# Hybrid two-layer trunk, one core: the odd layer's triangular inverse in 32x32 blocks, both output gates whole on ScalarE, and one output factor in the weight rows

## The reference

```python
m = jnp.where(strict, betac[..., :, None] * kk * gam, 0.0)          # 64x64, strictly lower, per head and chunk
rhs = jnp.concatenate([vc * betac[..., None], kc * (betac * jnp.exp(bc))[..., None]], axis=-1)
sol = lax.linalg.triangular_solve(m + jnp.eye(CHUNK), rhs, left_side=True, lower=True, unit_diagonal=True)
...
o = rms_norm(o, out_gain) * jax.nn.silu(z)                          # mixer C, gate z
o = head_group_norm(o, d_gain, d_bias) * jax.nn.silu(g)             # mixer D (retention), gate g
return jnp.concatenate([o_c, o_d], axis=-1) @ w_out
```

## Time and profile before

| | |
|---|---|
| median of 3 runs | 586.52 us (586.25 to 588.19) |
| profiled execution | 586.91 us, of which its span (first to last instruction) 584.7 us |
| granted TensorE clock, mean | 0.975 |
| PE busy over the span | 541.3 us (93%) |
| DVE, ACT, POOL busy | 328.9, 254.0, 81.4 us |
| DMA | 144.16 MB, mean 247 GB/s |
| inverse, levels 1 to 6 (first line 2467 to last 2490) | about 363.8 to 405.4 us |
| first output projection unit | 420.31 us |

### The profile page before, as it was taken

The page is one execution under the profiler, slowest core; times in us unless marked ns, Lnnn a source line. Parts: engine busy times, 40 slices in busy tenths (PEclk is TensorE's granted clock), DMA queues, the critical chain, the costliest instruction groups (busy, mean ns, idle before and its releaser), DMA issues.

```text
span 584.7 us, 12159 instructions
## 1 busy us (share of the span) xinstructions
PE 541.3 (93%) x5162; PEld 445.5 (76%) x5162; DVE 328.9 (56%) x595; ACT 254.0 (43%) x501; POOL 81.4 (14%) x98
## 2 busy tenths in 40 slices
PE   6999799999899999789999999999999889999975
PEld 6999799996565645359989998999889656664632
DVE  3579876657334333377996555467445633334335
ACT  5576467664233323155546434433226323331311
POOL 5716621100000000021003900011110000000000
PEclk9999999998999999999999799999789989999999
DMA  9991333787899999997463430000315979989992
GB/s 319 272 371 58 108 109 110 228 305 295 312 408 409 375 411 409 390 376 243 160 215 80 176 109 2 4 4 2 145 34 225 411 282 411 408 347 412 407 409 109
DMA packets 55671, 144.16 MB, mean 247 GB/s; under 512 B 4292, under 2 KB 29088, under 8 KB 55488
## 3 DMA queue, kind: packets, MB, share of 16 engines
q1 hardware_dynamic: 54496, 141.88, 64.6%
q0 software_dynamic: 944, 1.41, 1.2%
q10 hardware_dynamic: 176, 0.07, 0.1%
HBM read 142.30 MB, written 1.05 MB: 245 GB/s over the span
## 4 chain that ended last, share of the span: by engine, by line
PE 75%; DVE 14%; ACT 5%; issue 3%; POOL 1%; DMA 1%; ACTq 0%; DVEq 0%
PE PS L2097 11%; PE PS L2058 7%; PE PS L2119 6%; PE PS L610 6%; PE PS L611 5%; PE PS L612 5%; PE PS L2133 4%; PE PS L646 3%; DVE WL L606 3%; PE PS L648 2%; PE PS L647 2%; PE PS L2134 2%; PE PS L2467 2%; PE PS L2488 2%; DVE SL L1303 2%
## 5 line engine op out<-in xcount | busy, mean ns | idle before, releaser
L606 DVE TENSOR_TENSOR WL<-RAW,WH 128x768 fp32r<-128x768 f32 (+2 forms) x90 | 82.0, 947 | 30.2 <-ACT WH L592 29.8
L610 PE MATMUL PS<-WH,HTH 128*128 128x384 f32 (+2 forms) x272 | 93.2, 343 | 3.0 <-DVE HTL L1295 1.4
L611 PE MATMUL PS<-WL,HTH 128*128 128x384 f32 (+2 forms) x272 | 90.1, 331 | 0.0
L612 PE MATMUL PS<-WH,HTL 128*128 128x384 f32 (+2 forms) x272 | 90.0, 331 | 0.0
L1295 DVE TENSOR_TENSOR X<-PS,X 128x512 f32<-128x512 f32 (+2 forms) x84 | 53.9, 663 | 48.0 <-PE PS L2134 36.1
L592 ACT ACTIVATE WH<-RAW 128x768 fp32r<-128x768 f32 (+2 forms) x90 | 67.2, 793 | 4.8 <-PE PS L612 3.1
L610 PEld LDWEIGHTS PS<-WH,HTH 128*128 128x128 f32 x272 | 53.5, 197 | 4.4 <-DVE HTL L1295 1.7
L611 PEld LDWEIGHTS PS<-WL,HTH 128*128 128x128 f32 x272 | 53.7, 197 | 0.0
L992 ACT ACTIVATE SIL<-PS,MW 128x128 f32<-128x128 f32 x18 | 6.6, 367 | 107.6 <-PE PS L2097 98.0
L612 PEld LDWEIGHTS PS<-WH,HTL 128*128 128x128 f32 x272 | 53.3, 196 | 0.0
L646 PE MATMUL PS<-HTH,WH 128*128 128x256 f32 x160 | 46.0, 287 | 0.4 <-DVE HTL L1303 0.4
(11 more groups left out here) (362 smaller groups left out, 1060.8 us busy)
## 6 DMA issues: line engine op xcount, KB each, us to landing
RAW<-moe_w_down SPq DMA_DIRECT2D x32, 512.0 KB, 13.1
RAW<-moe_w_gate SPq DMA_DIRECT2D x32, 512.0 KB, 7.8
RAW<-moe_w_up SPq DMA_DIRECT2D x32, 512.0 KB, 8.6
XD<-moe_w_down SPq DMA_DIRECT2D x32, 512.0 KB, 13.4
XG<-moe_w_gate SPq DMA_DIRECT2D x32, 512.0 KB, 9.2
XG<-moe_w_up SPq DMA_DIRECT2D x32, 512.0 KB, 10.3
RAW<-od_w_in SPq DMA_DIRECT2D x9, 1536.0 KB, 7.8
RAW<-ev_w_in SPq DMA_DIRECT2D x5, 1536.0 KB, 15.4
```

The source lines that it names most:

```text
L606: done(nc.vector.tensor_tensor(out=lo, in0=raw, in1=hi.bitcast(F32), op=ALU.subtract), "unit_lo")
L610: nc.tensor.matmul(ps, ah, bh, start=start, stop=False)
L611: nc.tensor.matmul(ps, ah, bl, start=False, stop=False)
L612: return nc.tensor.matmul(ps, al, bh, start=False, stop=stop)
```

## The change

Three edits.

**The inverse.** Levels 1 to 4 work on 32x32 blocks, four to a column of 128 partitions (`quarters`), so that a call loads 32 columns of weights. Only half of a block's columns is needed as the right factor (`first_half`), 16 columns. The products of a level no longer depend on each other in a row: the transposes and the products of `NTD` with `YC` are issued together (`inverse_TQ`), one ACT copy of 128x384 takes both (`inverse_X`), and one product follows (`inverse_Z`). Two small masked copies (`placed`) bring it into `YC`. Level 0 now has a product of its own (`inverse_N`). Level 5 puts 64x64 blocks together with calls of 32 or 64 columns; level 6 (`inverse_last`, `inverse_last_Z`) keeps 64x64 calls and additionally transposes all of `YC` into `UT`, which ACT copies in quarters (`inverse_upper`). `solved` is then one 128x64 call per head instead of two. The two groups are staggered by one level.

**The gates.** ACT takes Silu of the whole gates; DVE no longer forms them.

**The factor.** Mixer C's gain is loaded as a column (`CCOLG`) and multiplied into the rows of the output weights when they are split; `CGAIN` and its DVE multiplication go. The table of masks grows from 7 to 10 slices.

```diff
@@ masks, split of the weights
+    lower = np.stack([upper[0:CH, n, 0:CH].T for n in range(6)], 1)
+    lower = np.concatenate([lower, lower], 0).reshape(P, 3, P)
+    return np.concatenate([upper, lower], 1).astype(np.float32)
...
+            if plan[i][:2] == (1, "out") and j < 2:
+                return CCOLG
...
@@ GpSimd
+            for i in range(NT):
+                link(nc.gpsimd.memset(UT[CH:P, 2 * i, :, 0:CH], 0.0), also="c_uz")
...
-                link(nc.gpsimd.tensor_copy(YS[CH:P, :, hs, :], YC[CH:P, :, hs, :]), also="c_ys")
@@ ScalarE
             def inverse_X(g, L):
-                rows = slice(0, P if L < 6 else CH)
                 act.wait_ge(sem(f"c_T{g}"), L)
-                done(nc.scalar.activation(heads(XC, g)[rows], level_ps(0, g)[rows], ACT.Copy), f"c_X{g}")
-
-            def inverse_Q(g, L):
-                rows = slice(0 if L < 6 else CH, P)
-                act.wait_ge(sem(f"c_Q{g}"), L)
-                done(nc.scalar.activation(heads(QC, g)[rows], level_ps(2, g)[rows], ACT.Copy), f"c_Qs{g}")
+                done(nc.scalar.activation(XC[:, g, :], PS[:, g, 0:384], ACT.Copy), f"c_X{g}")
...
+            def inverse_upper(g, c):
+                act.wait_ge(sem(f"c_T{g}"), 6)
+                rows = slice(CH * c, CH * c + CH)
+                done(nc.scalar.activation(UT[rows, 0::2, 4 * g:4 * g + 4, rows],
+                                          PS[rows, g, :].rearrange("p (h i t) -> p i h t", h=4, i=2), ACT.Copy), f"c_Qs{g}")
...
-            done(nc.scalar.activation(SG[:, :, :], TM[:, :, 0:512], ACT.Tanh, scale=0.5), "gate_t")
+            done(nc.scalar.activation(SG[:, :, :], TM[:, :, 0:512], ACT.Silu), "gate_t")
@@ VectorE
+            def placed(g, L, b):
+
+                c = 2 ** (L + 1)
+                for half in range(2):
+                    cols = slice(32 * half, 32 * half + 32)
+                    to = YC[:, 4 * g:4 * g + 4, :, cols].rearrange("p h i (m c) -> p (h i) m c", c=c)[:, :, :, 0:c // 2]
+                    m1 = MKC[:, L, cols].rearrange("p (m c) -> p m c", c=c)[:, :, 0:c // 2]
+                    z = PS[:, b, 0:128].rearrange("p (n m c) -> p n m c", n=8, c=c // 2)
+                    done(nc.vector.copy_predicated(to, m1.unsqueeze(1).to_broadcast([P, 8, 32 // c, c // 2]), z), f"c_Y{g}")
...
-            link(stt(tg, tg, 1.0, TM[:, :, 1552:2064], ADD, MUL))
-            link(stt(SG[:, :, :], SG[:, :, :], 1.0, TM[:, :, 0:512], ADD, MUL))
-            link(stt(g16, g16, 0.5, bc(CGAIN, 1, [P, 16, 64]), MUL, MUL))
@@ TensorE
+            def inverse_TQ(g, L):
+                pe.wait_ge(sem(f"c_Y{g}"), 2 * L)
+                if L < 5:
+                    for n, (i, h) in enumerate(group(g)):
+                        for q, rows in enumerate(quarters):
+                            mm(PS[rows, g, 32 * n:32 * n + 32], inverse_block(q, i, h), ident[rows, rows], start=True, stop=True)
+                    for n, (i, h) in enumerate(group(g)):
+                        o = 256 + 16 * n
+                        for q, rows in enumerate(quarters):
+                            last = mm(PS[rows, g, o:o + 16], key_block(q, i, h), first_half(inverse_block(q, i, h), L),
+                                      start=True, stop=True)
...
+            def inverse_Z(g, L):
+                pe.wait_ge(sem(f"c_X{g}"), L)
...
+                        for q, rows in enumerate(quarters):
+                            last = mm(PS[rows, 2 + 2 * g, 16 * n:16 * n + 16], XC[rows, g, 32 * n:32 * n + 32],
+                                      XC[rows, g, 256 + 16 * n:256 + 16 * n + 16], start=True, stop=True)
...
-                    mm(PS[low, 2 * i + g, hs], YC[low, i, h, :], rhs[low, h, :], start=True, stop=True)
-                    last = mm(PS[high, 2 * i + g, hs], YS[:, i, h, :], rhs[:, h, :], start=True, stop=True)
+                    last = mm(PS[:, 2 * i + g, hs], UT[:, 2 * i, h, :], rhs[:, h, :], start=True, stop=True)
```

More of the change, by code:

```diff
@@ L591, in split_hi, with row_gain @@
             raw, hi, _ = unit_views(i, j)
-            done(nc.scalar.activation(hi, raw, ACT.Copy, scale=BCOLG if scaled(i, j) else 1.0), "unit_hi")
-        def scaled(i, j):
-            return plan[i][:2] == (0, "out") and j >= 2
+            gain = row_gain(i, j)
+            done(nc.scalar.activation(hi, raw, ACT.Copy, scale=1.0 if gain is None else gain), "unit_hi")
+        def row_gain(i, j):
+            if plan[i][:2] == (0, "out") and j >= 2:
+                return BCOLG
+            if plan[i][:2] == (1, "out") and j < 2:
+                return CCOLG
+            return None
         def split_lo(dve, i, j):
@@ L1870, in _ @@
             inverse_level(0, 1)
+            first_level(1)
+            inverse_level(0, 2)
             inverse_level(1, 1)
@@ new lines, in _, with first_half, key_block, inverse_block @@
+            quarters = [slice(32 * q, 32 * q + 32) for q in range(4)]
+            def first_half(a, L):
+                return a.rearrange("p (m c) -> p m c", c=2 ** (L + 1))[:, :, 0:2 ** L]
+            def key_block(q, i, h):
+                return NTD[quarters[q], h, 256 * i + 32 * q:256 * i + 32 * q + 32]
+            def inverse_block(q, i, h):
+                return YC[quarters[q], h, i, 32 * (q % 2):32 * (q % 2) + 32]
+            def inverse_N(g):
+                pe.wait_ge(sem("c_nt"), 2 * g + 1)
+                for n, (i, h) in enumerate(group(g)):
+                    for q, rows in enumerate(quarters):
+                        last = mm(PS[rows, g, 16 * n:16 * n + 16], key_block(q, i, h), first_half(ident[rows, rows], 0),
+                                  start=True, stop=True)
+                done(last, f"c_N{g}")
@@ new lines, in inverse_Z, with inverse_last @@
+                done(last, f"c_Z{g}")
+            def inverse_last(g):
+                pe.wait_ge(sem(f"c_Y{g}"), 12)
+                for n, (i, h) in enumerate(group(g)):
+                    last = mm(PS[high, 2 + 2 * g, CH * n:CH * n + CH], NTD[low, h, 256 * i + CH:256 * i + P], YC[low, h, i, :],
+                              start=True, stop=True)
+                done(last, f"c_Q{g}")
+                for n, (i, h) in enumerate(group(g)):
+                    for rows in halves:
+                        last = mm(PS[rows, g, CH * n:CH * n + CH], YC[rows, h, i, :], ident[rows, rows], start=True, stop=True)
+                done(last, f"c_T{g}")
@@ L2491, in inverse_Z, with inverse_last_Z @@
+            def inverse_last_Z(g):
+                pe.wait_ge(sem(f"c_Qs{g}"), 2)
+                for n, (i, h) in enumerate(group(g)):
+                    last = mm(PS[low, 3 + 2 * g, CH * n:CH * n + CH], QC[high, g, n, :], UT[high, 2 * i, h, CH:P], start=True, stop=True)
                 done(last, f"c_Z{g}")
@@ L2531, in _ @@
             pe.wait_ge(sem("proj_ev"), proj_total[1])
+            inverse_N(0)
             key_scores(1)
+            inverse_TQ(0, 1)
             retention_scores(1)
[L2534 to L2547 removed]
+            pe.wait_ge(sem("c_nt"), 2)
+            inverse_Z(0, 1)
+            inverse_N(1)
+            inverse_TQ(0, 2)
+            inverse_TQ(1, 1)
+            retention_out()
+            inverse_Z(0, 2)
+            inverse_Z(1, 1)
+            inverse_TQ(0, 3)
+            inverse_TQ(1, 2)
+            inverse_Z(0, 3)
+            inverse_Z(1, 2)
+            values_T()
+            inverse_TQ(0, 4)
+            inverse_TQ(1, 3)
+            inverse_Z(0, 4)
+            inverse_Z(1, 3)
+            query_scores(0)
+            inverse_TQ(0, 5)
+            inverse_TQ(1, 4)
+            inverse_Z(0, 5)
+            inverse_Z(1, 4)
+            query_scores(1)
+            inverse_last(0)
+            inverse_TQ(1, 5)
+            inverse_last_Z(0)
+            inverse_Z(1, 5)
+            query_scores(2)
+            inverse_last(1)
             first_rows(0)
+            query_scores(3)
+            inverse_last_Z(1)
+            residue(0, 1)
             first_rows(1)
             pe.wait_ge(sem("c_at"), 4)
+            outputs(0, 0, 1)
+            second_rows(0)
+            residue(1, 2)
             lhs(mixed, lambda i: pe.wait_ge(sem("d_mix"), 1), D_PIECES)
[L2552 to L2555 removed]
             outputs(1, 0, 3)
```

216 lines of the change are left out of this document (97 added, 119 removed).

## The result

The changed kernel is slower: 605.9 us median of 6 runs (596.2 to 615.7) against 586.4 for the kernel before, ratio 1.0218 with a 95% interval of 1.017 to 1.0266. Forecast were 574 us and a range of 568 to 593. A second comparison on another chip gave 1.0186 (1.0108 to 1.0265).

A forecast was written before the change was run, and what follows sets the result against it. PE, issuing the inverse's products without a gap, was taken as the bound. Savings 16.3 - 1.7 - 2.0 + 2.2, plus 1.1 for the last solve, less 3.0 and 0.3, left 12.6 off 586.9: 574 us, range 568 to 593.

The forecast's parts named there:

- what a 32x32 call costs: Inverse on PE: a 32x32 call (two records) takes 15.5 ns with four corners, against 58.5 ns a call before.
- how fast PE takes records in: PE's intake, read from 48 layer 0 records on four corners: 24 ns a record or less.
- the 10.6 us to be saved: Levels 1 to 4 of the inverse: 5.62 us a level becomes 2.98, saving 4 x 2.64 us.
- Rival 2: Inverse: PE takes narrow records no faster than today; 58.5 ns a call, 608 us, or 50 ns, 601; chance 0.10.
- Corners: Inverse: the four diagonal 32x32 blocks run beside each other in the array, as four 64x64 corners do in layer 0.
- Rival 3: Inverse: only two corners run side by side, 29.3 ns a call, 582 us; chance 0.11.
- The clock: Before the first output unit: 3.0 us allowed for a clock fall; fails if at 0.50 for over 7 us.
- Rival 1: Small products leave PE so empty that its clock stays at 1.2 GHz through the inverse; 592 us, chance 0.12.
- Levels 0 and 5, the solve: PE: level 0 adds 1.0 us; level 5 falls from 5.62 to 2.4; each solve from 2.05 to 0.84 to 0.9.
- Copies: Inverse: ACT's 384-column copy takes 0.47 us, DVE's small masked copy of 128 elements 0.30.
- Rival 4: Inverse waits for DVE: a small masked copy takes 0.73 us, giving 581 us; chance 0.05.
- The rest: Outside the inverse: gates' table load hidden, gain folding 0 to 0.1 us, larger masks at the start cost 0.3 us.

The follow-up runs named there:

- the kernel in 64x64 calls: Changed kernel's order, transposed inverse, one-call solve and gates, but 64x64 calls at all levels; 1.0002 of the kernel before.
- 160 further calls: Kernel before plus 160 64x64 calls into idle array corners in the T (transpose) steps of levels 1 to 5, results unread; 1.0097 of the kernel before.
- 464 further calls: Kernel with 64x64 calls at all levels plus 464 calls into idle corners in T, Q and Z steps, results unread; 603.6 us, 1.0286 of the kernel before.
- half of the blocks: Changed kernel without the odd 32-row corners in levels 0 to 4, so half the blocks are not inverted; 577.7 us, 0.9925 of the kernel before.
- the values' transposes later: 64x64-call kernel with VectorE transposes, its TensorE transposes of the values moved behind the Q steps of levels 4 and 3; 0.9983 of the kernel before.

## Why the prediction was wrong, by its steps

- **The step that failed** is the cost of a call, 15.5 ns, under "what a 32x32 call costs", at "how fast PE takes records in: 24 ns or less, no more". The nearest row was 48 records long, 96 instructions: less than one packet. It could show the pace of a burst and nothing on the pace over 4000 instructions. In a burst at a clock of 1.00 the 15.5 was nearly right: at 380.35 us, 62 records of L2503 take 0.72 us and one alone 0.19, 8.7 ns apart, 17.4 a call. Sustained, a call is four instructions of 13.6 to 14.0 ns: 54.5 to 56 ns. At that price the 768 calls of levels 1 to 4 are 42 to 43 us (an estimate), where the 384 before were 22.5 and 11.9 were forecast: the 10.6 us to be saved became a loss.
- **The count** of instructions was never made. Between the last input product and the first output product TensorE has 2509 instructions before and 4317 after. At 14.0 ns the latter are 60 us by themselves, as long as the whole stretch was (61.1), so nothing was left to save. The trace of before does not show the limit, though: in it TensorE never stands still for want of a packet, and its packets start 3.7 us apart at the closest from 363 to 412. The count would have raised the question, not settled it.
- **Rival 2** had the place and the price (58.5 ns a call and 608 us, or 50 and 601; measured 54.5 to 56 and 596 to 603), and 0.10 of the chance. Its mechanism was partly wrong: not the engine's intake of narrow records, but the supply of instructions. The page cited for it ("TensorEngine Tiling (Array Packing)", "Instruction Overhead", of the Trainium skill) agrees in that 32 and 64 streamed columns cost 0.91 and 0.96 us for 32 records; its overhead did not set the pace, since four corners ran side by side at 8.7 ns a record.
- **Corners**: right. Rival 3 is out by the same row.
- **The clock**: allowance 3.0 us, a fall like the one at 416; wrong in size. From 364 to 422 the clock is 0.71 on average, so at 0.50 for some 34 us, where more than 7 was the sign of failing. Rival 1's mechanism is there as well, as a second loss. Of the 29 us by which the first output unit missed 405.5, 15.9 are "issue" waits up to 412; the other 13 are the clock and the order, which no run separates.
- **Levels 0 and 5, the solve**: level 0 was right, its 128 records stand 8.7 to 8.9 ns apart. Level 5 took 3.9 us in the chain instead of 2.4; its two T steps, 1.0 us each, stood at a clock of 0.50. The solve's four calls took 1.03 to 1.10 us instead of 0.9, without the pairs of 0.26; the long wait of `outputs` for the solution was 2.5 us (forecast 2.9). The solve's calls so became about 1 us shorter each time, as forecast; but the kernel in 64x64 calls has the same one-call solve and is as a whole no faster than the kernel before (1.0002), so that gain went elsewhere, which no run separates.
- **Copies**: 490 ns (forecast 470) and 348 (300). Rival 4 is out: ScalarE and VectorE waited for TensorE, 39 and 30 us.
- **The rest**: the gates' table load was hidden; from the first output unit on the kernel takes 163.2 us where before takes 164.7 (forecast 1.1 less). The masks land in 7.2 us instead of 6.5.

## What to carry to other kernels

Count TensorE's instructions over a stretch (two for each matmul record) and divide: here the packets allowed one per 14.0 to 15.2 ns, whatever the shape or the clock; only what had been fetched ahead passed faster, and in bursts. A change that makes matmuls smaller and more numerous gains nothing once the present stream is near that; this one was at 17.8 ns, and the doubled calls had nowhere to go. Read the DMA view for the instruction queue, and take an "issue" wait in the middle of an unbroken step for a missing packet if such waits stand 256 instructions apart; work that another engine can take off the list (a 128x512 transpose of 32x32 blocks, 712 ns on VectorE, for 16 calls) is then worth more than faster calls.

## What the runs showed of the hardware that was not expected

- Instructions for TensorE come in packets of 16 KB, 256 each, in the changed kernel 3.4 to 3.8 us apart at the limit, though a packet itself lasts only 0.9 to 1.4 us. About 1.1 us pass from TensorE going on to the start of the next packet, and 2.3 to 2.7 from there to TensorE going on again. Why it takes that long is open; there was no other DMA (5 GB/s in all).
- The limit did not follow the granted clock: 14.0 ns an instruction by the packets at an average of about 0.7 (changed kernel) and at 1.00 (160 further calls), 15.0 at 1.00 in the kernel with 464 further calls (up to 389.3). Within a packet narrow records did: 8.7 ns apart at 1.00 (380.35 us), 13.4 at 0.50 (369.49 us).
- The clock was 1.00 from 364 to 389 in the kernel before, in the 64x64 order and with 160 or 464 further calls. It was lower there in the others: 32x32 corners with stalls (0.71; 0.77 with wider streams, 0.70 with VectorE transposes), 32x32 corners with no stall to speak of (half of the blocks: 0.67), and 64x64 calls without stalls but 640 instructions fewer (0.80, and 0.77 with the values' transposes later). With 464 further calls it fell after 389, behind the stalls (0.66 from 402 to 412). So neither the narrow corners nor the stalls are needed for a fall; what decides it is open.
